# Two-block transformer on one core: the first two tiles of five stages multiplied before the norm, S5's products and two turns placed anew

## The reference

```python
def first_block(x, c, ...):
    cond = jax.nn.silu(c)
    for i in range(DEPTH):
        mod = cond @ ada_w[i] + ada_b[i]
        sh1, sc1, g1, sh2, sc2, g2 = jnp.split(mod[:, None, :], 6, axis=-1)
        h = rms_norm(x) * (1.0 + sc1) + sh1
        ...
            y = retention_mixer(h, pos, ret_w_in[j], ret_w_out[j])
        ...
            y = s5_mixer(h, s5_w_in[j], ..., s5_w_glu[j])
        x = x + g1 * y
        h = rms_norm(x) * (1.0 + sc2) + sh2
        x = x + g2 * conv_ffn(h, ffn_w_up[i], ffn_conv_w[i], ffn_conv_b[i], ffn_w_down[i])
    return rms_norm(x) * final_norm_g
```

## Time and profile before

| | us |
|---|---|
| runs of the kernel, median (lowest to highest of 3) | 3052.99 (3051.41 to 3059.58) |
| profiled execution, its own time | 3058.09 |
| its span, first to last instruction | 3056.3 |
| PE busy | 2941.5 |
| DVE busy | 1804.9 |
| ACT busy | 1103.6 |
| mean granted clock of TensorE | 0.973 |

### The profile page before, as it was taken

One profiled execution on the slowest core, in us unless ns is written; L12 is line 12 of the kernel. 1 busy time (PEld: TensorE's weight loads), 2 busy tenths in 40 slices (PEclk: granted clock), 3 DMA queues, 4 the chain that ended last, 5 costly groups with the idle time before them and its releaser, 6 DMA issues. The chain is left out here.

```text
span 3056.3 us, 37640 instructions
## 1 busy us (share of the span) xinstructions
PE 2941.5 (96%) x15078; PEld 2451.4 (80%) x15078; DVE 1804.9 (59%) x2518; ACT 1103.6 (36%) x1571; POOL 407.3 (13%) x390
## 2 busy tenths in 40 slices
PE   6999988999999999999999999999999899999999
PEld 5778767788878878888768878888998787778887
DVE  7456546766656567776636686664774437554443
ACT  3233234333332342324324432334553326442322
POOL 0100111686642100001000000000000103100000
PEclk9999999999998999999989999999999999999999
DMA  6434322455647455554414355543552431133332
GB/s 266 147 130 140 113 87 88 145 173 176 228 132 256 152 175 169 162 167 145 119 47 145 112 170 173 182 156 117 179 179 91 143 98 50 34 90 97 97 97 83
DMA packets 123310, 421.00 MB, mean 138 GB/s; under 512 B 21520, under 2 KB 21520, under 8 KB 122368
## 3 DMA queue, kind: packets, MB, share of 16 engines
q1 hardware_dynamic: 102096, 369.67, 38.5%
q0 software_dynamic: 11056, 41.95, 4.1%
q10 hardware_dynamic: 9984, 6.97, 0.7%
HBM read 401.31 MB, written 19.86 MB: 138 GB/s over the span
## 5 line engine op out<-in xcount | busy, mean ns | idle before, releaser
L121 DVE TENSOR_TENSOR wl<-raw,wh 128x1024 fp32r<-128x1024 f32 x506 | 659.3, 1303 | 554.6 <-ACT wh L118 531.4
L112 PE MATMUL bk<-HH,wh 128*128 128x512 f32 x2176 | 865.2, 398 | 22.3 <-DVE HL L133 13.4
L112 PE MATMUL bk<-HL,wh 128*128 128x512 f32 x2176 | 857.2, 394 | 0.0
L112 PE MATMUL bk<-HH,wl 128*128 128x512 f32 x2176 | 856.5, 394 | 0.0
L118 ACT ACTIVATE wh<-raw 128x1024 fp32r<-128x1024 f32 x506 | 531.1, 1051 | 429.7 <-PE bk L112 422.4
L112 PEld LDWEIGHTS bk<-HH,wh 128*128 128x128 f32 x2176 | 415.6, 191 | 115.9 <-DVE HL L133 16.0
L112 PEld LDWEIGHTS bk<-HL,wh 128*128 128x128 f32 x2176 | 416.1, 191 | 86.7 <-issue 1.0
L112 PEld LDWEIGHTS bk<-HH,wl 128*128 128x128 f32 x2176 | 414.8, 191 | 87.9
L124 DVE CUSTOM_DVE_ANT_0 ttr<-ar,cB 128x1024 f32<-128x1024 f32 x240 | 309.5, 1290 | 2.2
L112 PE MATMUL bk<-gh,wh 128*128 128x512 f32 x704 | 274.2, 389 | 0.0
L112 PE MATMUL bk<-gh,wl 128*128 128x512 f32 x704 | 273.9, 389 | 0.0
(11 more groups left out here) (301 smaller groups left out, 3881.6 us busy)
## 6 DMA issues: line engine op xcount, KB each, us to landing
raw<-in_wts_dram SPq DMA_DIRECT2D x506, 512.0 KB, 3.6
ar<-in_ada_dram SPq DMA_DIRECT2D x176, 512.0 KB, 4.3
first<-in_ada_dram SPq DMA_DIRECT2D x16, 512.0 KB, 15.3
F_d<-CA POOLq DMA_DIRECT2D x8, 512.0 KB, 5.0
E_d<-stg POOLq DMA_DIRECT2D x16, 256.0 KB, 4.2
M_d<-K_d POOLq DMA_DIRECT2D x8, 512.0 KB, 11.6
EB<-E_d POOLq DMA_DIRECT2D x8, 512.0 KB, 6.4
EB<-M_d POOLq DMA_DIRECT2D x8, 512.0 KB, 6.9
```

The source lines that it names most:

```text
L112: return Nothing() if self.e is None else self.e.matmul(*a, **k)
L121: return Nothing() if self.e is None else self.e.tensor_tensor(*a, **k)
```

## The change

At the five seams, `first_pair` multiplies the first two tiles by the parts of x(1 + scale), which `late_high` and `late_low` write tile by tile while the stage before still ends. The norm's sum stands behind step 1 of the pair, its turn behind step 3. Behind the pair stand 32 products of the same weights with the shift as a moving column (sh @ W). At the eviction DVE multiplies the two tiles by the root's row, copied to `rs` (`unscaled`), and the shift's result is added as a column (`shifts`). The other tiles use the normed HH and HL as before, made by `late_vec` and `late_act` meanwhile. For FFN 1 and FFN 3 they lie in new buffers HH1, HL1. In the even block, the final norm's turn stands behind the shift products (`fin_turn`).

In S5 the quarters' products and loads have a new order. Two turns of context norms stand one tile later. One knot of `KNOTS` moves from 138 to 142.

```diff
+        def first_pair(e, n, tag, w0, n_out):
+
+            u0 = open_units(tag, w0, n_out)
+            for k in range(8):
+                e.wait_ge(*act.of(("ph", n.tag, k)))
+                e.wait_ge(*vec.of(("pl", n.tag, k)))
+                c = slice(k * 128, k * 128 + 128)
+                for m in range(2):
...
+                    h, lo = wh[u % NH][:, c], wl[u % NH][:, c]
+                    e.matmul(b, h, n.hh[:, k, :], start=(k == 0), stop=False)
+                    e.matmul(b, h, n.hl[:, k, :], start=False, stop=False)
+                    mm = e.matmul(b, lo, n.hh[:, k, :], start=False, stop=(k == 7))
...
+                if k == 1:
+                    n.sum(e)
+                if k == 3:
+                    n.turn(e)
+            claim(e, 6)
+            e.wait_ge(*vec.of(("mod", n.ms, n.parts[0])))
+            for m in range(2):
+                u = u0 + m
+                for k in range(8):
+                    c = slice(k * 128, k * 128 + 128)
+                    shift = mod(n.ms, n.parts[0], k)
+                    e.matmul(BK[6][:, m:m + 1], wh[u % NH][:, c].bitcast(F), shift, start=(k == 0), stop=False)
+                    mm = e.matmul(BK[6][:, m:m + 1], wl[u % NH][:, c].bitcast(F), shift, start=False, stop=(k == 7))
+                mm.then_inc(*pe.up(("unit", u), *([("c", n.tag)] if m else [])))
...
-        KNOTS = ((0, 0), (2, 16), (12, 24), (58, 48), (76, 48), (122, 78), (138, 78), (152, 88), (214, 132), (222, 132), (240, 144), (260, 144), (318, 192), (600, 192))
+        KNOTS = ((0, 0), (2, 16), (12, 24), (58, 48), (76, 48), (122, 78), (142, 78), (152, 88), (214, 132), (222, 132), (240, 144), (260, 144), (318, 192), (600, 192))
...
+        def late_mods(e, n):
+            need_mod(e, n.ms, n.parts[0])
+            need_mod(e, n.ms, n.parts[1])
+
+        def late_vec(e, n, u, inverse=None, beside=lambda j: None):
+
+            late_low(e, n, 6)
+            late_low(e, n, 7)
+            (inverse or norm_inverse)(e, n)
+            norm_scaled(e, n, 0)
+            for j in range(8):
+                if j < 7:
+                    norm_scaled(e, n, j + 1)
+                norm_low(e, n, j)
+                if j == 4:
+                    lo(e, u + 2)
+                if j == 2:
+                    e.tensor_copy(rs[:, :], BK[n.b][:, :]).then_inc(*vec.up(("rb", n.tag)))
+                beside(j)
+                if j == 5:
+                    lo(e, u + 3)
+                    e.wait_ge(*pe.of(("c", n.tag)))
+                    e.tensor_copy(shifts, BK[6][:, 0:2]).then_inc(*vec.up(("c", n.tag)))
...
+        def unscaled(e, n, m, dst):
+
+            e.wait_ge(*pe.of(("pk", n.tag, 7)))
+            e.wait_ge(*vec.of(("rb", n.tag)))
+            e.tensor_tensor(dst, BK[m][:, :], rs[:, :], ALU.mult).then_inc(*vec.up(("ev", n.tag, m)))
...
             past(0)
             own(0)
-            run(g)
+            for _ in range(2):
+                next(g)
             past(1)
             own(1)
+            run(g)
+            past(2)
             out(0)
-            past(2)
-            own(2)
             out(1)
             past(3)
+            own(2)
             own(3)
...
+            late_mods(e, n_f1)
             for m in range(8):
                 lo(e, base["glu", m] + 3)
...
+                if 1 <= m < 7:
+                    late_low(e, n_f1, m - 1)
...
-            ffn_pe(e, f2, lambda e, *key: norm_turn(e, n_cf2, 4) if key == ("up", 2) else None)
+            ffn_pe(e, f2, lambda e, *key: norm_turn(e, n_cf2, 4) if key == ("up", 3) else None)
...
-            ffn_pe(e, fc, lambda e, *key: norm_turn(e, n_o, 5) if key == ("up", 2) else None)
+            ffn_pe(e, fc, lambda e, *key: norm_turn(e, n_o, 5) if key == ("up", 3) else None)
...
+            late_vec(e, n_e, base["e", "in"], twin_inverse)
+            norm_inverse(e, n_fin)
```

More of the change, by code:

```diff
@@ L419, in build, with norm @@
         st_.n = 0
-        def norm(tag, src, t, hh, hl, ms, parts, war, direct=False, columns=False, b=5):
+        def norm(tag, src, t, hh, hl, ms, parts, war, direct=False, columns=False, b=5, late=False):
             n = Space()
+            n.late = late
+            n.scaled_by = ("mod", ms, parts[1]) if parts else None
+            n.gain = lambda j: mod(ms, parts[1], j)
+            n.sum = lambda e: norm_sum(e, n, b)
+            n.turn = lambda e: norm_turn(e, n, b)
             n.direct, n.columns = direct, columns
@@ L499, in norm_inverse, with late_high, late_low @@
             e.reciprocal(n.st, n.st).then_inc(*vec.up(("rs", n.tag)))
+        def late_high(e, n, j, done, name):
+            e.wait_ge(*done.of(name))
+            e.wait_ge(*vec.of(n.scaled_by))
+            for other, before in n.free:
+                e.wait_ge(*other.of(before))
+            e.activation(n.hh[:, j, :], n.src[:, j, :], ACT.Copy, scale=n.gain(j)).then_inc(*act.up(("ph", n.tag, j)))
+        def late_low(e, n, j):
+            e.wait_ge(*act.of(("ph", n.tag, j)))
+            e.scalar_tensor_tensor(out=n.hl[:, j, :], in0=n.src[:, j, :], scalar=n.gain(j), in1=n.hh[:, j, :].bitcast(F),
+                                   op0=ALU.mult, op1=ALU.subtract).then_inc(*vec.up(("pl", n.tag, j)))
@@ L722, in ret_pe @@
                     turned(3)
-            run(out(3))
+            run(out(3, [0, 1, 2, 3]))
             end(pe, "ret")
@@ L933, in ret_vec @@
             gated(3, base[("out", 3)])
-            out(3)
+            late_mods(e, n_f0)
+            for m in range(8):
+                lo(e, last_unit(("out", 3), m, 4) + 2)
+                add_to(e, ("out", 3), m, m % 4, X, L, 0, 2)
+                if 1 <= m < 7:
+                    late_low(e, n_f0, m - 1)
             end(vec, "ret")
@@ L961, in ffn @@
             f.war = own or []
+            f.then = n_e if nxt is n_fin else nxt if nxt is not None and nxt.late else None
             return f
@@ L1037, in ffn_vec @@
                 need_mod(e, f.ms, 5)
+                then = f.then if bi == len(f.blocks) - 1 else None
+                if then is not None:
+                    late_mods(e, then)
+                    if then is n_e:
+                        make_gains(e)
                 for m in range(8):
@@ L1040, in ffn_vec @@
                     add_to(e, (f.tag, "dn", bi), m, m % 4, f.x, t, f.ms, 5)
+                    if then is not None and 1 <= m < 7:
+                        late_low(e, then, m - 1)
             end(vec, f.tag)
@@ L1431, in s5_act @@
                 norm_square(e, n_f1, m, vec, ("x", "glu", m))
+                if m < 7:
+                    late_high(e, n_f1, m, vec, ("x", "glu", m))
             end(act, "s5")
         def s5_vec(e):
-            norm_vec(e, n_s5)
+            late_vec(e, n_s5, base["s5u"], None, lambda j: [unscaled(e, n_s5, m, pr[m][:, :]) for m in range(2)] if j == 3 else None)
             def scan(qr):
@@ L1529, in build @@
         n_fin = norm("fin", X, L, None, None, None, None, [])
-        n_e = norm("e", X, L, HH, HL, 2, (0, 1), [], b=4)
-        both = nst[:, 96:100]
+        n_e = norm("e", X, L, HH, HL, 2, (0, 1), [], b=4, late=True)
+        n_e.free = [(pe, (("f1", "up", NF - 1), 1))]
+        n_e.last = ("x", ("f1", "dn", len(BLOCKS) - 1), 7)
         gains = nst[:, 104:112]
+        n_e.scaled_by = "gains"
+        n_e.gain = lambda j: gains[:, j:j + 1]
         sqg = rs
@@ L1740, in even_vec @@
             tag, t, nt, hn = v.tag, v.t, v.nt, v.hn
+            if hn.late:
+                for m in range(2):
+                    unscaled(e, hn, m, pr[m][:, :])
             for m in range(8):
```

221 lines of the change are left out of this document (140 added, 81 removed).

## The result

The changed kernel takes 3095.48 us (median of 4 runs, 3090.49 to 3103.31) against 3056.28 (3051.41 to 3060.91) for the one before on the same chip: ratio 1.0125, 95% interval 1.0098 to 1.0151. The forecast was 3089 us.

What follows compares the result with a forecast made beforehand. TensorE, busy 2941.5 of 3056.3 us, was taken as the bound. Seams +36.9 (-50.4 + 27.1 + 60.2), FFN 0 +2.5, ten steps +20.5, S5 -13.0 and turns -10.9 gave +36.0, so 3089 us; range 3062 to 3110.

Steps and rivals of the forecast that it cites:

- That is the most that the new seams could win: Five old seams: waits and low clock lose 50.4 us in all, the upper limit of the gain.
- the +27.1 that stays: New seams: token sums, turn, their clock and the even block's wait still cost 15.7 + 11.4 us.
- The root hides: In the pair at each seam: sum and two steps, 2.7 + 2.7 us, cover the root's 5 us.
- One group costs 12.1 us, and five 60.2: Shift products behind each pair: 7.2 us for 64 records at full clock plus 4.9 for the clock.
- has no gap in which to hide them: Shift products behind the pair: TensorE pays for all 64 records, 7.2 us at full clock.
- FFN 0, +2.5: Behind FFN 0's seam: VectorE reaches the first convolution some 4 us later behind TensorE, costing 2.5 us.
- Ten steps, +20.5: Before the glu: ten mod steps in a row make TensorE wait 19.9 us, then start slow; +20.5 us.
- S5, -13: S5's new order: from the end of tile 3 to the glu 66.3 us instead of 79.3.
- 1.5 for a short fall of the clock: In S5's stepped-through order: 1.5 us allowed for low clock, included in the 66.3 us.
- Turns, -10.9: FFN 2 and context FFN, turns one tile later: waits of 5.45 and 2.92 us and 2.7 of low clock hidden.
- The even block: Seam before the even block: 14.2 us lost before, 11.4 kept (3.6 for `fin_turn`), plus one group of 12.1.
- two rules weighed in the prediction: Skill rules against the group's price: clock falls only when TensorE idles (five groups 36 us); small products cost about 25 ns.

Runs made afterwards that it cites:

- the bare kernel: The changed kernel with 4 of the 32 shift products at each of the five seams (k = 0 alone): 3082.20 us, ratio 1.0092.
- the knot: The changed kernel with one knot at (137, 88) instead of (142, 78), so ten mod steps come due earlier: 3078.34 us, ratio 1.0075.

## Why the prediction held, and where it did not

The time and the sign were right, and so was the size of each seam: the forecast's five seams with FFN 0's tables are 36.9 + 2.5 = +39.4 us, measured +40.2. Their make-up was wrong, in two steps, and that these cancel is luck. In the rest of the sum S5 came out 8.2 us worse than forecast and the turns 3.5 better, which cancels in part too. A few of the sums are off in their last digits (5 x 12.1 is 60.5, the three terms of the turns give 11.1, and 1.2 + 4.3 less an overlap can't be 5.6); none moves the forecast by more than 0.5 us.

1. *"That is the most that the new seams could win": the -50.4 and the +27.1 that stays.* The step that failed is "The root hides". It does, but the normed parts of the third tile don't: they start at the turn, and VectorE needs over 12 us for eight scalings, eight low parts and a split (the last of them are still waited for at 494.41 with the turn at 480.83). I took the pair as long enough a cover. Without the group I would have had -50.4 + 27.1 + 2.5 and 4 for its last records, about -17; the bare kernel's seams are +1.8 + 3.6 + 2.6 + 6.2 + 2.5 = +16.6. So some 33 us were missing; 15.5 of them are the new waits for `wl` and 5.8 the longer one at `fin_turn`. The rest includes low clock: in windows of 30 us from the start of each seam (40 in the even block) the bare kernel has granted shares of 0.89, 0.83, 0.83, 0.79 and 0.89, which is 25.2 us of missing full speed where my sum had 5.2. Some of it lies over the waits, and no run took the two apart.
2. *"One group costs 12.1 us, and five 60.2".* Its length was right (9.1 to 10.7 us in the group and a low clock behind it), and a second one costs 13.6. But its first part fills the wait of step 1: taking 56 of 64 records out of five seams gave 23.6 us, where my sum has 53. The runs bear the reading out: the five groups take 50.0 us in the changed kernel, seven eighths of it are 43.7, and less the 21.3 us of waits that open without them this leaves 22.4. That TensorE "has no gap in which to hide them" was true of before, not of the changed kernel.
3. *FFN 0, +2.5.* Seam and tables together are +5.9 where 8.3 were expected. The waits for `wl` there remain; not tested apart.
4. *Ten steps, +20.5.* +20.0, and 20.2 given back by the knot. From the first step to the end of the last are 24.8 us (24.9 in the sum), 4.9 to 5.6 from pair to pair; TensorE waits 19.3 for it.
5. *S5, -13.* -4.8 in the profiled pair and nothing alone. The term that was mis-sized is "1.5 for a short fall of the clock": the rest came out in sum as stepped through (66.3 expected, 66.4 in a run in which the clock stayed up, though there the 2 us wait of quarter 0 is missing and one of 3.57 stands ahead of quarter 3's E products), but in the changed kernel the clock lies at 1.2 GHz from 983.6 to the end of S5, which loses 11 us. In nine of twelve profiles with the new order it fell so among the last groups (S5 takes 74 to 87 us), in three it stayed up: 66.4, and 72.9 and 72.6 with waits for `Ux` of 4.8 and 6.5 us at S5's start. The old order has 79.1 and 73.1. What sets the clock there is open. The three have the knot, but two others with the knot fell, and all seven without it. Waits inside the last E and M groups add up to 0 to 0.5 us in the three and to 0.9 to 2.6 in eight of the nine, but to 0.2 in the ninth. A wait ahead of them as such doesn't do it: two of the three have one of over 3 us.
6. *Turns, -10.9.* -14.4 and, alone, -13.6. Waits of 8.4 us for `nst` in that stretch are gone as predicted, and so is the low clock behind the first (2.7). The other 2.5 us of the turns alone are 1.7 us of shorter waits for `tm` and 0.9 of clock, which I did not take into the sum.
7. *The even block,* 9.3 expected, +11.5. The wait at `fin_turn` was 2.6 for the 3.6 expected; the low clock around it (PEclk 0.70 in its window) cost more.

Of the two rules weighed in the prediction, the first did not hold here: the clock fell inside groups without a gap. The second did not give the price: a record of one column costs 0.112 us at full and 0.213 at half clock. The floor of 25 ns that the Trainium skill ("TensorE: Matmul & The Clock Gate", section "Back-to-back issue gap") gives is that of an isolated product; the same section says that in a stream of weight loads and products both set the spacing, which the prediction left out when it weighed the floor. No run here tells the two apart.

The late seams do not pay even when nearly all shift products are left out. What paid in this change is the two turns, two lines, -14 us.

## What to carry to other kernels

A wait that is filled is not a wait that is removed: before an added group of work is priced at its length, follow the engine that feeds the next step (here VectorE, from the turn to the third tile's parts), and price only what goes past it. Taking the work out and doubling it give the two slopes, and here they differ by two and a half to one. A step that ends earlier may only wait for the next input, as S5 did for `Ux`. Where a number that rests on a state (a clock level that comes and goes in one stage) carries a term, give that term both values.

## What the runs showed of the hardware

- The clock fell to 1.2 GHz inside a group of one-column products with no idle time before or in it (FFN 0's group began at 487.29; the granted share is 0.50 from 492.20 to its end).
- One-column products mixed with wide ones ran at 1.2 GHz for 29 us in which TensorE was never idle (PEclk 0.51), but in one seam of five. In the other four the mix had 0.73 to 0.81, much as the windows with groups (0.70 to 0.82). I had expected the mix to be the better; what made that one seam differ is open.
- A product in f32 with one moving column leaves two records, one in the split type with two columns one, each 0.112 us at full clock: for these small products the number of records is the price.
- S5's last 256 records of 63 and 64 columns took 18 us in one run and 28 in another of kernels that have the same instructions there, at granted shares of 0.92 and 0.61. The slower one has 2.4 us of waits inside them; no run told what sets the clock.
